# Twenty-two taps of a depthwise convolution moved from VectorE to GpSimd, beside a recurrence

## The chip, the cores and the metric

The kernel runs on one core of one Trainium2 chip. The metric is the device time of one execution in microseconds. Engine names are those of the profile: PE is TensorE, DVE is VectorE, ACT is ScalarE, POOL is GpSimd, SP is SyncE, which only issues transfers here.

## The reference

One inference layer for 512 prompt tokens and 8 sample tokens, width 1024. Cut to what matters here:

```python
z = x @ w_in
u = z_conv[..., :512] * sigmoid(z_conv[..., 512:])          # GLU, 512 channels
c = depthwise_causal_conv(u, conv_w, width 31) + conv_b     # the convolution of this case
c = silu(layer_norm(c))
...                                                         # r, k, v, decay, rate, gate from the other columns
S_t = S_{t-1} diag(w_t) + (S_{t-1} a_t) b_t^T + v_t k_t^T   # RWKV-7 recurrence, 8 heads of 64
y_t = S_t r_t
h = concat(c, groupnorm(y) and bonus, gated) @ w_out
x = layer_norm(ALPHA * x + h);  x = layer_norm(ALPHA * x + moe(x))   # 64 experts, top 8
```

## The kernel before

All data is float32. The kernel has two blocks of instructions per engine. In the first (`prepare`) the input projection, the GLU, the token shift and the keys are made, and a small triangular system is solved on DVE. In the second (`recur_and_mix`) the recurrence runs over 16 chunks of 32 tokens, then come the normalisations, the output projection, the routing and the 64 experts.

The convolution lies in four tiles of 128 channels (`m.conv[:, i]`), each with 31 taps over 512 positions. `Taps.take(count)` does the next `count` taps on DVE. Tap 0 of a tile is one `tensor_scalar` (times weight, plus bias, L174), each other tap one `scalar_tensor_tensor` that multiplies the shifted input by the weight and adds the sum so far (L176). Each waits for the one before it (`Chain.link`). Of the 124 taps, 74 are done in the first block, 19 at the start of the second (14, then `add_reads(0)`, then 5, then `add_reads(1)`), and these complete the third tile. The fourth tile's 31 taps are spread over the recurrence: three in each of steps 0 to 9, and the last one in step 10 (`TAPS_OVER`).

A step `n` of the recurrence on DVE is, in order: the old state times the chunk's decay (L2025), plus `moves` (L2027), then side work that the step's tables name (`add_reads` L1973, `centre` L1924 to L1926, `shift_late` L1965, the taps, parts of the sample's state L1983 to L1992, and so on), then the wait for PE's `step(n)` and the addition of its product (L2062), which raises `state_ready`. PE's `step(n)` (L1455) waits for the state before it. Behind it PE's queue holds, in an order written out by hand, two late projection columns (L1583, in steps 1 and 3), `push` (L1406), `solve` (L1415), `moves_of` (L1431 to L1443) and `outputs` (L1469 to L1478); ACT copies their results out of PSUM (L1704 to L1721) before DVE and PE can use them. In step 10 DVE also finishes the convolution of the 8 sample tokens, and in step 11 it folds the four tiles for the mean (L1930, L1931), for which PE waits in step 12.

POOL's queue in the second block begins with clearing the 42 semaphores of the first block; then it waits for the last `solve` (`w2_done`), makes two small masks (L1366 to L1371), and has nothing further to do before the mixing is over. SP's queue issues the load of `w_out` (L1284) after the last late column and the last `solve`.

`place(m, at, ...)` and `view(...)` name pieces of large SBUF areas; `m.AT_COL` is where the projection's four weight buffers lie, of which the late columns use the second and third, and `pushed` the first half of the fourth.

Of the kernel before, what the change touches and what calls it, by code (L numbers as in the profile page):

```python
# [19 lines left out]
ALU = mybir.AluOpType  # L20
# [3 lines left out]
P = 128  # L24
D = 1024
KD = D // P
T = 512
# [4 lines left out]
DC = 512  # L32
CT = DC // P
# [43 lines left out]
WB = 4  # L77
# [14 lines left out]
def par(name):  # L92
    return CW + PARAMS.index(name)
# [30 lines left out]
def place(m, at, *shape):  # L124

    size = 1
    for n in shape:
        size *= n
    assert at + size <= SLOTS * EXPERT_FLOATS
    names = "abcde"[:len(shape)]  # L130
    flat = m.w_exp[:, at:at + size]
    return flat.rearrange(f"p ({' '.join(names)}) -> p {' '.join(names)}", **dict(zip(names, shape)))


def view(t, at, *shape):

    size = 1
    for n in shape:
        size *= n
    names = "abcde"[:len(shape)]  # L140
    return t[:, at:at + size].rearrange(f"p ({' '.join(names)}) -> p {' '.join(names)}", **dict(zip(names, shape)))


def halves(ap):

    return ap.rearrange("p (b t) -> p b t", b=2)
# [858 lines left out]
def recur_and_mix(nc, m, ctx_out):  # L1005
# [12 lines left out]
    TURN = {14: 0}  # L1018
    SCALE = {9: 0, 13: 1, 15: 3}
    TAPS_OVER = 10  # L1020
    CONV = 11
    BIG = 1e30
    GONE = -3e38
    QD = D // 4
    with ExitStack() as ctx:
# [3 lines left out]
        def sem(name):  # L1029
            return ctx_out.enter_context(nc.semaphore(name))  # L1030
# [5 lines left out]
        st = place(m, m.UPPER, 32, N)  # L1036
        ln_scale = place(m, m.AT_LORA, TT)
        w1 = m.glu_sig[:, 0:DC]
        state = view(m.x_area, 0, RING, CT, N)
        pushed = place(m, m.AT_COL + (WB - 1) * KD * P, DC)  # L1040
        tail_rows = view(m.x_area, RING * CT * N + DC, 2, DC)[0:38]
# [79 lines left out]
        def early_sem(name):  # L1121
            m.spent_later.append(m.second_sems.enter_context(nc.semaphore(name)))
            return m.spent_later[-1]
# [30 lines left out]
        bonus_scaled = sem("bonus_scaled")  # L1154
        o_ready = sem("o_ready")
        final_stored = sem("final_stored")
        conv_folded = early_sem("conv_folded")
        mean_done = early_sem("mean_done")
        conv_centred = early_sem("conv_centred")
# [77 lines left out]
        def tail_width(t):  # L1237
            return sum(column(*SHIFTED[s])[1] for s in tail_columns(t))
# [11 lines left out]
        with nc.Block() as block:  # L1250
            @block.sync
            def _(sp):
# [15 lines left out]
                for t in range(5):  # L1268
# [4 lines left out]
                    else:  # L1273
                        c0, w = DC * (t - 1), tail_width(t)
# [5 lines left out]
                sp.dma_start(sample_y, m.scr_y).then_inc(sample_y_loaded, 16)  # L1280
                sp.wait_ge(row_taken, use["col", 2 * LATE - 1] + 1)
                sp.wait_ge(w2_done, TM)
                for c in range(2):
                    sp.dma_start(m.w_out_half[c][:], m.w_out[:, c * 512:(c + 1) * 512].rearrange("(k p) n -> p k n", p=P)).then_inc(m.w_out_loaded[c], 16)  # L1284
                sp.dma_start(router_w[:], m.router_w.rearrange("(k p) n -> p k n", p=P)).then_inc(loaded, 16)
# [73 lines left out]
            @block.gpsimd  # L1359
            def _(pool):  # L1360
                for spent in m.spent:
                    pool.sem_clear(spent)
                pool.sem_inc(spent_cleared)
                ch = Chain(pool, m.pool_step, m.pool_count)
                pool.wait_ge(w2_done, TM)
                nc.gpsimd.memset(before[:], 1.0)  # L1366
                ch.link(nc.gpsimd.memset(first[:], 1.0))

                nc.gpsimd.affine_select(out=before[:], in_=before[:], compare_op=ALU.is_gt, fill=0.0, base=0,
                                        pattern=[[1, P]], channel_multiplier=-1)  # L1370
                nc.gpsimd.affine_select(out=first[:], in_=first[:], compare_op=ALU.is_gt, fill=0.0, base=0,  # L1371
                                        pattern=[[1, G], [-1, G]], channel_multiplier=0).then_inc(routing_consts, 1)
                pool.wait_ge(mixed, NT)
                nc.gpsimd.memset(scores[:, TM, :], 0.0).then_inc(routing_consts, 1)  # L1374
                pool.wait_ge(sh_sig_ready, 1)
                ch.link(nc.gpsimd.tensor_tensor(sh_sig[:], sh_sig[:], sh_gate[:], ALU.mult))
                pool.wait_ge(sh_up_ready, 1)
                nc.gpsimd.tensor_tensor(sh_h[:, 0, :], sh_sig[:], sh_h[:, 0, :], ALU.mult).then_inc(sh_h_ready, 1)
                pool.wait_ge(sh_sig_ready, 2)
                ch.link(nc.gpsimd.tensor_tensor(sh_sig[:], sh_sig[:], sh_gate[:], ALU.mult))  # L1380
                for b in range(2):
                    pool.wait_ge(sh_up_ready, 2 + b)
                    half = slice(HALF * b, HALF * (b + 1))
                    nc.gpsimd.tensor_tensor(sh_h[:, 1, half], sh_sig[:, half], sh_h[:, 1, half], ALU.mult).then_inc(sh_h_ready, 1)
                pool.wait_ge(x1_stored, 16 * NT)
                pool.wait_ge(sh_done, 8)
                for q in range(NB):
                    gather(nc, m, pool, Job(q))
                work.gpsimd(pool)

            @block.tensor
            def _(pe):
# [200 lines left out]
                for n in range(NCH):  # L1593
                    j, c = n // CM, n % CM
                    step(n)
                    if n == CONV + 1:
                        pe.wait_ge(conv_folded, 1)
# [98 lines left out]
            def _(act):  # L1696
# [98 lines left out]
                for n in range(NCH):  # L1795
# [27 lines left out]
                    if n in SCALE:  # L1823
                        scale_bonus(SCALE[n])
                    if n == CONV + 3:
                        act.wait_ge(conv_centred, 1)
# [80 lines left out]
            def _(dve):  # L1907
                ch = Chain(dve, m.vector_step, m.vector_count)
# [60 lines left out]
                def add_reads(g):  # L1969

                    dve.wait_ge(move_taken, g + 1)
                    r = m.r_dec[:, :, N * g:N * (g + 1)].rearrange("p i (c t) -> p c i t", c=2)
                    tt(r, r, p_keep[:, :, :, N:], ALU.add).then_inc(read_taken, 1)  # L1973
# [45 lines left out]
                for n in range(NCH):  # L2019
                    j, c = n // CM, n % CM  # L2020
                    old, new = state[:, n % RING], state[:, (n + 1) % RING]
                    dve.wait_ge(state_ready, n + 1)
                    if n + 1 >= RING:
                        dve.wait_ge(y_done, (n + 1 - RING) // CM + 1)
                    ch.link(tt(new, old, m.chunk_decay[:, :, n:n + 1].broadcast_to([P, CT, N]), ALU.mult))  # L2025
                    dve.wait_ge(move_taken, n // 2 + 1)
                    ch.link(tt(new, new, moves[:, (n // 2) % SETS, n % 2, 1].rearrange("p (i n) -> p i n", i=CT), ALU.add))  # L2027
                    if c == 3 and j + 1 < TM:
                        add_reads(2 * j + 2)
                    if c == 0 and j >= 1:  # L2030
                        add_reads(2 * j + 1)
                    if n in INVERT:
                        invert(INVERT[n])
                    if n in FINISH:
                        finish_out(FINISH[n])
                    if n in CENTRE:
                        centre(CENTRE[n])
                    if n in SHIFT:
                        shift_late(SHIFT[n])
                    if n < TAPS_OVER:  # L2040
                        taps.take(min(3, CT * CW - m.taps_done))
                    if n < 2:
                        sample_reads(n)
                    elif n < 4:
                        sample_kept_part(n - 2)
                    elif n == 4:
                        sample_rows_out()
                    if n == TAPS_OVER:
                        taps.take(CT * CW - m.taps_done)
                        ch.link(tt(m.conv[:, :, T:TT], m.u_pad[:, :, CW - 1 + T:CW - 1 + TT], m.params[:, :, CW - 1:CW].broadcast_to([P, CT, B]), ALU.mult))  # L2050
                        ch.link(tt(m.conv[:, :, T:TT], m.conv[:, :, T:TT], m.conv_sum[:], ALU.add))
                    if n == CONV:
                        fold_chunks(m.conv)
                    if n == CONV + 2:
                        dve.wait_ge(mean_done, 1)
                        for i in range(CT):
                            last = tt(halves(m.conv[:, i, :]), halves(m.conv[:, i, :]), banks(p_sum), ALU.subtract)
                        last.then_inc(conv_centred, 1)
                    if n in SUM:
                        squares(SUM[n])  # L2060
                    dve.wait_ge(step_done, n + 1)
                    tt(new, new, pst[:], ALU.add).then_inc(state_ready, 1)  # L2062
# [75 lines left out]
                ch.link(nc.vector.tensor_tensor(sel_g, sel_g, keep_f, ALU.mult))  # L2138
                ch.link(nc.vector.tensor_scalar(grp[:], keep[:], 1.0, BIG, ALU.subtract, ALU.mult))
                ch.link(nc.vector.tensor_tensor(sel_g, sel_g, grp_f.unsqueeze(2).broadcast_to([P, NT * G, E // G]), ALU.add))  # L2140
# [838 lines left out]
```

## Time and profile before

| | us |
|---|---|
| median of 3 runs | 1148.97 |
| lowest and highest | 1143.69, 1150.23 |
| the profiled execution: its own time | 1149.05 |
| the profiled execution: its span | 1147.3 |
| start of the second block (PE's first instruction in it) | 221.5 |
| steps 0 to 7 of the recurrence on DVE | 240.48 to 287.14 |
| steps 8 to 15 on DVE | 287.14 to 328 |
| experts | 467 to 1111 |

The span is cut into stretches by time from its start. In a row of the timeline the first number is the start, the second the length of the instruction or of several alike in a row (x3), and the bracket behind it the time for which the engine had been idle before, and what ended it. On one engine the rows can overlap by some 0.08 us, since the end of an instruction overlaps the start of the next one.

### The profile page before, as it was taken

The numbers are of one execution on the slowest core, as the hardware profiler recorded it, in microseconds if no ns is written. First come the engines' busy times: TensorE is split into PE (matmuls) and PEld (weight loads), VectorE is DVE, ScalarE is ACT, GpSimd is POOL, SyncE is SP. The second block draws the span as 40 slices with busy tenths as digits, with TensorE's granted clock in tenths as the row PEclk, the third lists the DMA queues.
The fourth block names the chain that finished last, engine by engine and source line by source line (L and its number), as shares of the span: only waits on it lengthen the run. The fifth ranks groups of instructions, "written<-read, shape, count | busy, mean of one in ns | idle before, by whom it ended". The sixth has DMA issues, their size and how long they took to land.

```text
span 1147.3 us, 31310 instructions
## 1 busy us (share of the span) xinstructions
PE 1063.6 (93%) x13702; PEld 753.5 (66%) x13703; DVE 714.2 (62%) x1562; ACT 224.7 (20%) x472; POOL 320.9 (28%) x327
## 2 busy tenths in 40 slices
PE   7999998977889999999999999999999999999996
PEld 6877886755653577666666666666666666666662
DVE  0788869788674869755586455544454544555438
ACT  2146421222447121010011110011101011100113
POOL 2000010000000002454455444444444444444410
PEclk9998999979669999999999999999999999999998
DMA  7221131330435467699999999999999999999661
GB/s 214 74 56 38 54 93 42 75 120 5 161 101 199 148 233 297 240 363 367 359 366 367 380 360 356 377 350 359 370 360 357 361 361 356 365 372 350 184 180 76
DMA packets 91928, 282.44 MB, mean 246 GB/s; under 512 B 22494, under 2 KB 49631, under 8 KB 66949
## 3 DMA queue, kind: packets, MB, share of 16 engines
q1 hardware_dynamic: 74685, 243.55, 57.0%
q0 software_dynamic: 16160, 33.62, 11.9%
q10 hardware_dynamic: 944, 3.24, 0.8%
q8 instruction: 109, 1.79, 0.6%
q14 instruction: 30, 0.25, 0.1%
HBM read 260.93 MB, written 35.86 MB: 259 GB/s over the span
## 4 chain that ended last, share of the span: by engine, by line
PE 64%; DVE 9%; issue 4%; ACT 2%; DMA 1%; SPq 0%; DVEq 0%; POOLq 0%
PE ph L2364 32%; PE ph L2391 19%; PE ph L1542 2%; PE ph L1560 2%; PE pz_late L1583 1%; DVE w_exp L176 1%; PE ph L1683 1%; DMA w_exp<-scr_f 1%; DVE w_exp L2602 1%; PE pz_late L1500 1%; DVE w_exp L2594 1%; PE pz_late L1501 1%; DMA scr_f<-arena,row 1%; PE ph L1431 1%; PE pt L933 0%
## 5 line engine op out<-in xcount | busy, mean ns | idle before, releaser
L2364 PEld LDWEIGHTS ph<-arena,w_exp 128*64 128x64 f32 x8192 | 353.1, 138 | 103.2 <-issue 100.5
L2364 PE MATMUL ph<-arena,w_exp 128*64 128x96 f32 x8192 | 389.6, 248 | 30.6 <-issue 26.6
L2391 PE MATMUL ph<-w_exp,arena 128*96 128x512 f32 x512 | 234.6, 601 | 0.0
L977 POOL DMA_INDIRECT x_area<-scr_x,piece_row x192 | 203.4, 1060 | 82.8 <-issue 56.4
L2426 POOL DMA_INDIRECT scr_f<-arena,row x62 | 91.6, 1477 | 265.7 <-PE ph L2364 236.9
L523 PE MATMUL pz<-w_exp 128*128 128x260 f32 x672 | 159.0, 395 | 0.3 <-ACT w_exp L335 0.3
L2391 PEld LDWEIGHTS ph<-w_exp,arena 128*96 128x96 f32 x512 | 78.4, 162 | 109.9 <-issue 103.2
L523 PEld LDWEIGHTS pz<-w_exp 128*128 128x128 f32 x672 | 129.9, 196 | 23.7 <-issue 2.7
L2409 DVE TENSOR_SCALAR arena<-ph,row_weight 96x512 f32<-96x512 f32 x64 | 47.8, 747 | 130.8 <-PE ph L2391 130.8
L2379 DVE TENSOR_TENSOR arena<-arena,ph 128x192 f32<-128x192 f32 x64 | 22.5, 352 | 161.3 <-ACT arena L2372 161.3
L2372 ACT ACTIVATE arena<-ph 128x192 f32<-128x192 f32 x64 | 21.1, 330 | 479.9 <-PE ph L2364 464.8
L2349 DVE STREAM_TRANSPOSE arena<-x_area 128x768 f32<-128x768 f32 x64 | 102.5, 1601 | 3.2 <-DMA x_area<-scr_x,piece_row 2.0
L176 DVE SCALAR_TENSOR_TENSOR w_exp<-arena,w_exp 128x512 f32<-128x512 f32 x120 | 90.0, 750 | 3.6
L2401 ACT ACTIVATE arena<-ph,row_weight 96x512 f32<-96x512 f32 x64 | 43.6, 682 | 104.0 <-PE ph L2391 76.7
L1560 PE MATMUL ph<-w_exp 128*128 128x512 f32 x128 | 57.8, 604 | 0.0
L1560 PEld LDWEIGHTS ph<-w_exp 128*128 128x128 f32 x128 | 24.2, 194 | 29.5 <-issue 29.0
L955 DVE TENSOR_SCALAR piece_row<-found 32x3 uint32<-32x3 f32 x240 | 40.6, 169 | 4.4
L964 DVE COPY row_weight<-found 32x2 f32<-32x2 f32 x180 | 36.9, 205 | 3.1
L809 POOL COPY w_exp<-w_exp 128x8 f32<-128x8 f32 x4 | 2.6, 653 | 129.2 <-DVE w_exp L727 129.2
L922 DVE TENSOR_TENSOR arena<-slot_index,position 128x480 bf16<-128x480 f32 x60 | 38.4, 644 | 0.0
L1374 POOL MEMSET arena<- 128x64 f32 x1 | 0.2, 151 | 115.7 <-PE ph L1572 115.7
L1366 POOL MEMSET arena<- 128x128 f32 x1 | 0.2, 204 | 106.0 <-PE ph L1415 106.0
(384 smaller groups left out, 1016.7 us busy)
## 6 DMA issues: line engine op xcount, KB each, us to landing
w_exp<-in_exp_up_dram SPq DMA_DIRECT2D x64, 1024.0 KB
w_exp<-in_exp_down_dram SPq DMA_DIRECT2D x64, 1024.0 KB
w_exp<-in_exp_gate_dram SPq DMA_DIRECT2D x64, 1024.0 KB
w_exp<-in_w_in_dram SPq DMA_DIRECT2D x22, 512.0 KB, 3.9
w_exp<-in_x_prompt_dram SPq DMA_DIRECT2D x8, 512.0 KB, 5.4
w_exp<-in_w_out_dram SPq DMA_DIRECT2D x2, 2048.0 KB, 11.6
w_exp<-scr_f SPq DMA_DIRECT2D x8, 512.0 KB, 8.5
x_area<-scr_x,piece_row POOLq DMA_INDIRECT x192
```

Source lines behind the costliest of these rows:

```text
L176: self.ch.link(self.nc.vector.scalar_tensor_tensor(out, u, w, out, ALU.mult, ALU.add))
L523: last = nc.tensor.matmul(banks(pz[0:w, c % 2, :])[:, b, :], m.w_col[:, c % WB, k, 0:w], halves(m.x_t[:, k, :])[:, b, :], start=(k == 0), ...
L922: nc.vector.tensor_tensor(m.members[:, e], m.slot_index[:].unsqueeze(1).broadcast_to([P, NT, CAP]), src.unsqueeze(2).broadcast_to([P, NT, ...
L955: last = nc.vector.tensor_scalar(m.piece_row[32 * quad:32 * (quad + 1), s, :], m.found[rows, :, 0], float(QUADS), float(QUADS * TT + quad) ...
L977: nc.gpsimd.indirect_dma_start(m.x_pieces[:, s, r, :], None, m.scr_x1.rearrange("t (q c) -> (t q) c", q=QUADS), bass.IndirectOffsetOnAxis( ...
L1560: last = nc.tensor.matmul(ph[0:n, i % 2, c * 512:(c + 1) * 512], lhs, w_out[c][:, kw, :], start=(part == 0 and k == 0), stop=(part == 1 an ...
L2349: nc.vector.transpose(x_list_t[:, s % 2].rearrange("p k (r t) -> p r k t", r=RUNS), m.x_pieces[:, s].rearrange("p r (c k) -> p r k c", k=K ...
L2364: last = nc.tensor.matmul(pgu[64 * half:64 * half + 64, s % 2, (2 * part + j) * CAP:(2 * part + j + 1) * CAP], w[job.slot][:, k, f0:P * ha ...
L2391: last = nc.tensor.matmul(pyl[0:CAP, c, :], hid[:, s % 2, j, :], m.expert_down[job.slot][:, j, c * 512:(c + 1) * 512], start=(j == 0), sto ...
L2401: nc.scalar.activation(y_list[:, s % 2, 0:512], pyl[0:CAP, 0, :], ACT.Copy, scale=row_weight[0:CAP, job.l, 1:2]).then_inc(y_act, 1)
L2409: nc.vector.tensor_scalar(y_list[:, s % 2, 512:1024], pyl[0:CAP, 1, :], row_weight[0:CAP, job.l, 1:2], None, ALU.mult).then_inc(y_dve, 1)
L2426: nc.gpsimd.indirect_dma_start(m.scr_f[copy_of(q)], bass.IndirectOffsetOnAxis(ap=row[:, job.l:job.l + 1], axis=0), y_list[:, s % 2, :], No ...
```

## The change

POOL does the first 22 taps of the fourth tile, in the second block, before its wait for `w2_done`. A tap is two instructions there: a `tensor_scalar` into one of two buffers (`tap_product`, in the first weight buffer, which is free by then), and a `tensor_tensor` that adds this to the sum. Tap 0 is one `tensor_scalar`. DVE takes no taps in steps 0 to 7; in steps 8, 9 and 10 it takes three each, after a wait in step 8 for all 22. SP's load of `w_out` waits for them too, since it overwrites the buffers.

```diff
@@ recur_and_mix
     TAPS_OVER = 10
+    POOL_OVER = (8, 9)
     CONV = 11
+    LAST_TILE = CT - 1
+    POOL_TAPS = 22
+    PRODUCTS = 2
...
+        tap_product = [place(m, m.AT_COL + at, T) for at in (0, T, (WB - 1) * KD * P + DC)][0:PRODUCTS]
...
+        taps_added = sem("taps_added")
... SP's queue
                 sp.wait_ge(w2_done, TM)
+                sp.wait_ge(taps_added, POOL_TAPS)
                 for c in range(2):
                     sp.dma_start(m.w_out_half[c][:], ...)
... POOL's queue
                 pool.sem_inc(spent_cleared)
                 ch = Chain(pool, m.pool_step, m.pool_count)
+                sums = m.conv[:, LAST_TILE, 0:T]
+                for k in range(POOL_TAPS):
+                    u, w = m.u_pad[:, LAST_TILE, k:k + T], m.params[:, LAST_TILE, k:k + 1]
+                    if k == 0:
+                        bias = m.params[:, LAST_TILE, par("conv_b"):par("conv_b") + 1]
+                        nc.gpsimd.tensor_scalar(sums, u, w, bias, ALU.mult, ALU.add).then_inc(taps_added, 1)
+                    else:
+                        product = tap_product[k % PRODUCTS]
+                        ch.link(nc.gpsimd.tensor_scalar(product, u, w, None, ALU.mult))
+                        pool.wait_ge(taps_added, k)
+                        nc.gpsimd.tensor_tensor(sums, sums, product, ALU.add).then_inc(taps_added, 1)
                 pool.wait_ge(w2_done, TM)
... DVE's queue, step n
-                    if n < TAPS_OVER:
+                    if n in POOL_OVER:
+                        if n == POOL_OVER[0]:
+                            dve.wait_ge(taps_added, POOL_TAPS)
+                            m.taps_done += POOL_TAPS
                         taps.take(min(3, CT * CW - m.taps_done))
```

## Rows read from the trace of the kernel before

**Rows 1.** Windows: busy us and instructions of each engine, PE's clock, DMA share.

```profile
core 0: us, PE busy (x) PEld busy (x) DVE busy (x) ACT busy (x) POOL busy (x), PEclk, DMA share, GB/s
221.50:240.40 18.90, 16.25 (x388) 13.99 (x392) 15.10 (x23) 5.38 (x12) 0.00 (x0) 0.92 0.70 227
240.40:287.10 46.70, 36.35 (x984) 26.04 (x974) 42.98 (x72) 11.84 (x24) 0.00 (x0) 0.83 0.03 6
...
467.00:1100.00 633.00, 602.39 (x8742) 422.06 (x8735) 336.24 (x890) 64.08 (x128) 286.65 (x248) 1.00 0.97 346
```

**Rows 2.** Timeline of DVE, from the second block's start to step 0.

```profile
221.99 10.89 DVE L176 SCALAR_TENSOR_TENSOR w_exp<-arena,w_exp 128x512 f32<-128x512 f32 x14
234.87 0.42 DVE L1973 TENSOR_TENSOR w_exp<-w_exp,ph 128x256 f32<-128x256 f32 x1 [1.99 <-ACT w_exp L1721]
235.21 3.90 DVE L176 SCALAR_TENSOR_TENSOR w_exp<-arena,w_exp 128x512 f32<-128x512 f32 x5
240.14 0.42 DVE L1973 TENSOR_TENSOR w_exp<-w_exp,ph 128x256 f32<-128x256 f32 x1 [1.04 <-ACT w_exp L1721]
```

**Rows 3.** Timeline of DVE, steps 1, 4, 8 and 11.

```profile
247.43 2.33 DVE L176 SCALAR_TENSOR_TENSOR w_exp<-arena,w_exp 128x512 f32<-128x512 f32 x3
...
251.06 1.22 DVE L1984 TENSOR_REDUCE arena<-arena 128x16 f32<-128x1024 f32 x1
...
269.11 0.42 DVE L1973 TENSOR_TENSOR w_exp<-w_exp,ph 128x256 f32<-128x256 f32 x1 [1.64 <-ACT w_exp L1721]
...
288.41 0.42 DVE L1973 TENSOR_TENSOR w_exp<-w_exp,ph 128x256 f32<-128x256 f32 x1 [0.39 <-ACT w_exp L1721]
...
305.98 0.42 DVE L2062 TENSOR_TENSOR x_area<-x_area,pst 128x256 f32<-128x256 f32 x1 [1.96 <-PE pst L1455]
```

**Rows 4.** Timeline of PE: the late column of step 3, and step 11.

```profile
260.73 5.38 PE L1583 MATMUL pz_late<-w_exp 128*32 128x260 f32 x16
...
304.83 1.12 PE L1455 MATMUL pst<-x_area,w_exp 64*64 64x64 f32 x16 [4.35 <-issue]
```

**Rows 5.** Groups of POOL's instructions by shape: busy us, mean ns, idle before.

```profile
L2780 POOL TENSOR_SCALAR_AFFINE_SELECT w_exp<-w_exp 128x128 f32<-128x128 f32 x3 | 0.9, 311 | 0.2
...
L2767 POOL MEMSET arena<- 128x512 f32 x1 | 0.5, 517 | 0.0
...
L2786 POOL TENSOR_SCALAR_AFFINE_SELECT is_token<-is_token 128x1 f32<-128x1 f32 x1 | 0.2, 186 | 0.0
```

**Rows 6.** Timeline of POOL: shared expert, beside DVE's work.

```profile
433.28 1.28 POOL L1376 TENSOR_TENSOR arena<-arena 128x520 f32<-128x520 f32 x1 [19.03 <-ACT arena L1883]
...
448.21 1.16 POOL L1384 TENSOR_TENSOR arena<-arena 128x260 f32<-128x260 f32 x1 [2.24 <-ACT arena L1890]
451.65 0.73 POOL L1384 TENSOR_TENSOR arena<-arena 128x260 f32<-128x260 f32 x1 [2.28 <-ACT arena L1890]
```

**Rows 7.** Timeline of DVE: two collisions, and a small TENSOR_TENSOR in step 2.

```profile
256.78 0.23 DVE L1990 TENSOR_TENSOR arena<-arena 128x64 f32<-128x64 f32 x1
...
433.57 1.08 DVE L2127 TENSOR_TENSOR arena<-arena 128x40 f32<-128x40 f32 x1
...
448.06 0.71 DVE L2165 TENSOR_TENSOR arena<-arena,table 128x320 f32<-128x320 f32 x1
```

**Rows 8.** Timeline of POOL: small copies of the first block, then its first mask.

```profile
79.75 0.65 POOL L809 COPY w_exp<-w_exp 128x8 f32<-128x8 f32 x1 [70.14 <-DVE w_exp L727]
80.35 0.66 POOL L810 COPY w_exp<-w_exp 128x8 f32<-128x8 f32 x1
...
81.54 0.18 POOL L813 COPY w_exp<-w_exp 128x8 f32<-128x8 f32 x1
...
297.51 0.20 POOL L1366 MEMSET arena<- 128x128 f32 x1 [105.97 <-PE ph L1415]
```

**Rows 9.** Timeline of DVE beside those copies.

```profile
79.68 0.67 DVE L732 TENSOR_TENSOR w_exp<-w_exp,arena 128x496 f32<-128x496 f32 x1
80.27 0.69 DVE L734 TENSOR_TENSOR x_area<-w_exp 128x512 f32<-128x512 f32 x1
```

## The prediction

> **What bounds the kernel now.** I read the windows first. From 467 us on PE is busy for 602 of 633 us at full granted clock [rows 1], and that stretch starts when everything before it is done, so a time gained or lost earlier is gained or lost at the end, one for one. The change lies in two windows. From 221.5 to 240.4 us DVE is busy for 15.1 of 18.9 us, and from 240.4 to 287.1, steps 0 to 7, for 42.98 of 46.7; PE has 36.35 there, at a mean clock of 0.83, and POOL has nothing [rows 1]. So DVE is what limits steps 0 to 7, and POOL is free.
>
> The timeline of DVE shows where that time goes. Ahead of step 0 stand 14 and 5 taps with two waits for ACT behind them, 1.99 and 1.04 us [rows 2]. In a step the three taps are 2.33 us of some 6 [rows 3]. DVE's waits inside the stretch are few: 1.64 us in step 4, behind the late column of step 3 on PE [rows 3, 4], and 0.39 at the start of step 8 [rows 3]. In step 11 DVE waits 1.96 us for PE, which itself had stood idle for 4.35 us for no cause that the profile names ("issue") [rows 3, 4].
>
> **What is removed.** Steps 0 to 7 held 24 taps; step 10 goes from one to three. A tap costs its start-to-start distance, 10.89/14 = 0.78 us [rows 2]. So 24 x 0.78, less 0.2 for the shorter first one, is 18.5 us off DVE in steps 0 to 7, and 2 x 0.78 = 1.6 us on in step 10, at most. If nothing else happened, the gain could not be 18.5: PE's 36.35 us of work in that window leave 10.3 of the 46.7 [rows 1], and the taps now cover PE and ACT's work in steps 3 and 7, whose waits would grow.
>
> **What is added on POOL.** 22 one-input multiplications and 21 additions with two inputs, of 128x512. An addition of 128x520 alone took 1.28 us, one of 128x260 0.73 [rows 6], so 2.1 ns per element and 0.18 fixed: 1.26 us for 512. For the multiplication there is no row. Below it lies the memset of 512, 0.52 us; above it the two-input addition, 1.26. Nearest is the affine select, one input and one output as well: 0.31 us for 128 elements against 0.19 for one, 0.98 ns per element, so 0.19 + 512 x 0.98 = 0.69 [rows 5]. I take 0.65 to 0.7, and keep both ends. Alone the chain is 22 x 0.68 + 21 x 1.26 + 43 x 0.06 for the links = 44 us. POOL starts behind 42 semaphore clears, for which no row has a price: nothing, or at most 42 x 0.19 (the smallest instruction in [rows 5]), 8 us. I take 1.5, so a start at 223, and an end at 267 if it met no one. DVE reaches step 8 at 287, so its wait there is 20 us away, and SP's wait for the taps stays hidden too: the last `solve`, for which it waits anyway, ends at 297.5 [rows 8].
>
> **What the two engines do to each other.** This is the part that decides. In the shared expert POOL's addition ran from 433.28 to 434.56 [rows 6]. DVE's TENSOR_TENSOR of only 40 elements, started at 433.57, took 1.08 us and ended at 434.65 [rows 7]; one of 64 elements takes 0.23 [rows 7]. It stood until POOL was done. The other way round, DVE had a TENSOR_TENSOR from 448.06 to 448.77 [rows 7] and POOL's addition of 260 elements, started at 448.21, took 1.16 us instead of 0.73 [rows 6]. So the two exclude each other for nearly the whole of an instruction. Who wins in a row of DVE instructions is in the first block: copies of 8 elements on POOL take 0.18 us alone and 0.65 and 0.66 beside DVE, each ending as one DVE instruction ends [rows 8, 9]. They take turns; neither starves. After a turn some 0.15 us of the waiting instruction's fixed part is already over, as the 1.08 us above shows (0.09 left after POOL's end, against 0.23).
>
> A tap on DVE is a SCALAR_TENSOR_TENSOR with two inputs in SBUF; no row shows that form beside POOL. By the nearest rows it is blocked as TENSOR_TENSOR is; the bound below is that it is not blocked at all. The Trainium skill says more than these rows (SBUF — State Buffer, Who interferes with whom): any VectorE instruction with two SBUF inputs contends with a GpSimd instruction that reads SBUF, whichever starts first keeps the port for its whole length, and a reduce does not contend. By that rule taps would be blocked and the sum below would stand; were only TENSOR_TENSOR blocked, the first term of it would be gone. On the multiplication's price the skill (GPSIMD Engine Reference, Engine selection) calls one-input work roughly line rate, with which the row of the affine select agrees.
>
> **The sum.** When each met instruction takes turns, POOL's hold the way for their length less some 0.15 us: 0.5 for a multiplication, 1.1 for an addition, 0.8 on average; DVE gets back 0.15 of it. So a DVE instruction with two SBUF inputs is 0.65 us later for each POOL instruction it meets.
> - Up to step 0: 18 of the 19 taps meet one, 18 x 0.65 = 11.7 us, less the 3.03 us that DVE waited for ACT anyway: step 0 starts 8.7 us later, with about 20 of POOL's 43 done.
> - Steps 0 to 7: 18.5 us of taps gone. The other 23 POOL instructions meet some 28 two-input instructions of DVE, but where DVE reduces one input (1.22 us, once in each of steps 0 to 3 [rows 3]), reads PSUM or waits, they cost nothing; I take two in three as met, 15 x 0.65 = 10 us. The waits behind the late columns in steps 3 and 4, formerly covered by taps, come to some 3 us. Net -5.5.
> - Start of step 8: PE's and ACT's moves, which step 7's taps had covered, now show; the 0.39 us wait becomes about 2, +1.5.
> - Step 10: 1.6 us, which PE's 4.35 us pause in step 11 should hide, since DVE waits 1.96 us for it [rows 3, 4]. 0, or 1.6 if the pause moves.
> - PE, waiting longer before step 0, starts from the lower of its two clocks more often; it was at a mean of 0.83 already [rows 1]. +1, from nothing to 3.
>
> 8.7 - 5.5 + 1.5 + 0 + 1 = +5.7, say +6. The profiled execution took 1149.05 us, by 1.75 more than its span and within 0.1 of the median. So 1155.
>
> **The rivals.**
> - *Less met, or a cheap multiplication* (0.52 us, the memset's row, or a later start of POOL): the multiplications hold 0.15 less, 22 x 2/3 x 0.15 = 2.2 us, a start 4 us later leaves some 5 collisions fewer ahead of step 0, 3 us. Together +1: 1150. It shows as step 0 at 245 or earlier.
> - *A dear multiplication*, as long as an addition, 1.26: 0.55 more in each, 22 x 0.55 = 12 us on POOL, of which some two thirds are met: +8. The chain is then 56 us alone and, with some 15 us of waiting for DVE, ends at 294, so that DVE also stands at step 8. +14: 1163. Against it: the affine select.
> - *No collision with taps* (other side). If SCALAR_TENSOR_TENSOR leaves POOL its way, the 8.7 us ahead of step 0 don't arise, POOL is half through by step 0, and steps 0 to 7 give what PE leaves, 10.3 at most, less 1.5 at step 8 and what the steps' own TENSOR_TENSORs lose. -8 at best, -6 likely: 1142. It decides from this: a loss ahead of step 0 under 3 us, which is the slack there. Against it: both collisions in the trace.
>
> **Chances.** About 0.5% or 5.7 us is what a measurement of this kernel can tell from no change. Forecast (+3 to +9): 0.50, about half of it beyond the bound. Less met (-3 to +3): 0.16. Dear multiplication (+9 to +16): 0.22. No collision with taps (-10 to -3): 0.12. So faster 0.10, same 0.41, slower 0.49. The likeliest case's own range is 1152 to 1158; the range that holds eight in ten runs from 1145 to 1163.
>
> **What would show it.** Right: DVE's 14 taps from 222 us stretch from 10.9 to about 20 us, their mean near 1.4; step 0 starts near 249; a POOL addition in there takes 1.5 to 1.9 us, start to end; POOL is done near 280, without DVE waiting for it at step 8; step 8 starts 3 us later than before, the experts 5 to 6 later. Wrong: taps at 0.75 us beside POOL, or POOL's multiplications over 1 us where DVE is idle, or step 8 starting before 285. If the loss is there ahead of step 0 but the experts start no later, then the steps had more to give than I allowed.

## The result, and the profile after

| | median us (executions) | against the kernel before, same chip |
|---|---|---|
| before | 1148.69 (20), from 1143.69 to 1152.32 | |
| changed | 1153.12 (20), from 1148.65 to 1156.61 | 1.0042 [1.0029, 1.0055] |

The change makes the kernel slower by 0.42%, 4.8 us at 1148.69 (the two medians themselves are 4.4 us apart); forecast were 1155 us and +6. The size was right. The sum behind it was not: its first term was four to five times too large, and a wait of 6 us that it denied made up for that. That the two nearly cancel is in good part luck.

The profiled execution took 1155.57 us, its span 1153.6. The windows of the changed kernel: the stretch ahead of step 0, steps 0 to 7, and the experts (columns as in [rows 1]).

```profile
221.12:242.30 21.18, 18.84 (x435) 15.76 (x436) 20.34 (x23) 5.70 (x13) 17.35 (x11) 0.85 0.62 203
242.30:282.20 39.90, 31.32 (x839) 22.25 (x841) 31.48 (x49) 10.88 (x23) 38.90 (x26) 0.88 0.03 6
467.30:1117.80 650.50, 613.75 (x8989) 432.81 (x8988) 337.64 (x892) 64.44 (x129) 289.05 (x249) 1.00 0.96 341
```

The block starts at 221.12, so step 0 is 21.2 us behind it, where it was 19.0 [rows 1]. POOL began only 11 instructions in that time. Steps 0 to 7 take 39.9 us instead of 46.7; POOL is busy for all of it and DVE no longer is: 31.48 us against 42.98. The timeline of DVE, ahead of step 0 and in step 8:

```profile
221.61 14.89 DVE L176 SCALAR_TENSOR_TENSOR w_exp<-arena,w_exp 128x512 f32<-128x512 f32 x14
236.54 0.42 DVE L1991 TENSOR_TENSOR w_exp<-w_exp,ph 128x256 f32<-128x256 f32 x1
236.88 5.09 DVE L176 SCALAR_TENSOR_TENSOR w_exp<-arena,w_exp 128x512 f32<-128x512 f32 x5
242.00 0.42 DVE L1991 TENSOR_TENSOR w_exp<-w_exp,ph 128x256 f32<-128x256 f32 x1
242.34 1.03 DVE L2043 TENSOR_TENSOR x_area<-x_area 128x256 f32<-128x256 f32 x1
...
282.18 0.42 DVE L2043 TENSOR_TENSOR x_area<-x_area 128x256 f32<-128x256 f32 x1
282.64 0.42 DVE L2045 TENSOR_TENSOR x_area<-x_area,w_exp 128x256 f32<-128x256 f32 x1
286.46 0.42 DVE L1991 TENSOR_TENSOR w_exp<-w_exp,ph 128x256 f32<-128x256 f32 x1 [3.40 <-ACT w_exp L1739]
292.90 2.33 DVE L176 SCALAR_TENSOR_TENSOR w_exp<-arena,w_exp 128x512 f32<-128x512 f32 x3 [6.02 <-POOL w_exp L1382]
...
296.32 0.43 DVE L2043 TENSOR_TENSOR x_area<-x_area 128x256 f32<-128x256 f32 x1
```

L2043 is the first instruction of a step (L2025 before). The 14 and 5 taps grew from 10.89 and 3.90 us [rows 2] to 14.89 and 5.09, and both waits for ACT between them are gone. Step 8 lasts 14.1 us (5.0 before): DVE waits 3.40 us for ACT (0.39 in [rows 3]), then 6.02 us for POOL's last addition. The timeline of POOL, at its start and at its end:

```profile
224.53 0.76 POOL L1377 TENSOR_SCALAR w_exp<-arena 128x512 f32<-128x512 f32 x1 [35.21 <-issue]
225.28 2.00 POOL L1380 TENSOR_SCALAR w_exp<-arena 128x512 f32<-128x512 f32 x1
227.36 1.48 POOL L1382 TENSOR_TENSOR w_exp<-w_exp 128x512 f32<-128x512 f32 x1
228.83 1.99 POOL L1380 TENSOR_SCALAR w_exp<-arena 128x512 f32<-128x512 f32 x1
230.90 1.50 POOL L1382 TENSOR_TENSOR w_exp<-w_exp 128x512 f32<-128x512 f32 x1
...
289.96 1.56 POOL L1380 TENSOR_SCALAR w_exp<-arena 128x512 f32<-128x512 f32 x1
291.60 1.27 POOL L1382 TENSOR_TENSOR w_exp<-w_exp 128x512 f32<-128x512 f32 x1
```

The last rows fall in DVE's wait, so they are the prices without company: 1.27 us for the addition, as forecast, and 1.56 for the multiplication, where I had 0.65 to 0.7. Beside taps it is 2.00. Tap 0 multiplies and adds in one instruction and takes 0.76. Single taps on DVE, and pairs of them (x2), where the second row of a pair starts with the second tap:

```profile
222.30 0.75 DVE L176 SCALAR_TENSOR_TENSOR w_exp<-arena,w_exp 128x512 f32<-128x512 f32 x1
...
229.43 1.06 DVE L176 SCALAR_TENSOR_TENSOR w_exp<-arena,w_exp 128x512 f32<-128x512 f32 x1
...
230.52 2.43 DVE L176 SCALAR_TENSOR_TENSOR w_exp<-arena,w_exp 128x512 f32<-128x512 f32 x2
...
231.31 2.74 DVE L176 SCALAR_TENSOR_TENSOR w_exp<-arena,w_exp 128x512 f32<-128x512 f32 x2
```

The one at 222.30 met nothing. The one at 229.43 began and ended inside POOL's multiplication from 228.83 to 230.82 and was held for 0.31 us. The next began at 230.52, and the one after it, which the last row names, at 231.31, inside the addition from 230.90 to 232.40. That one ended at 230.52 + 2.43 = 232.95, 1.64 us after its start: held for 0.89. By the Trainium skill (SBUF — State Buffer, Who interferes with whom) whichever of two such instructions starts first keeps the port for its whole length. The addition agrees, with one tap read. The multiplication does not: by the rule the tap at 229.43 would have ended after 230.82, and it ended at 230.49.

### The profile page after: what moved, and what is told of

Same layout as the page of the kernel before. It is cut to its first block, busy times and chain, and to the rows that moved or that the text cites. A ratio compares the mean times of both kernels' runs of the same rounds, so it can differ in the third digit from the quotient of the medians.

```text
span 1153.6 us, 31349 instructions
## 1 busy us (share of the span) xinstructions
PE 1063.3 (92%) x13702; PEld 754.2 (65%) x13703; DVE 709.0 (61%) x1540; ACT 224.7 (19%) x472; POOL 387.8 (34%) x370
## 4 chain that ended last, share of the span: by engine, by line
PE 60%; DVE 7%; POOL 6%; issue 4%; ACT 1%; DMA 1%; POOLq 0%; SPq 0%; DVEq 0%
PE ph L2385 32%; PE ph L2412 19%; POOL w_exp L1380 3%; POOL w_exp L1382 3%; PE ph L1560 2%; PE ph L1578 2%; PE ph L1701 1%; DMA w_exp<-scr_f 1%; DVE w_exp L176 1%; DVE w_exp L2623 1%; PE pz_late L1518 1%; DMA scr_f<-arena,row 1%; DVE w_exp L2615 1%; PE pz_late L1519 1%; PE pt L933 0%
## 5 line engine op out<-in xcount | busy, mean ns | idle before, releaser
L176 DVE SCALAR_TENSOR_TENSOR w_exp<-arena,w_exp 128x512 f32<-128x512 f32 x99 | 79.4, 802 | 9.1 <-POOL w_exp L1382 6.0
L1380 POOL TENSOR_SCALAR w_exp<-arena 128x512 f32<-128x512 f32 x21 | 35.3, 1683 | 0.0
```

The costliest lines, as they stand in the source:

```text
L176: self.ch.link(self.nc.vector.scalar_tensor_tensor(out, u, w, out, ALU.mult, ALU.add))
L1380: ch.link(nc.gpsimd.tensor_scalar(product, u, w, None, ALU.mult))
```

## The experiments

Ratios are to the kernel before on the same chip, with 95% intervals. They are not the quotients of the two medians, from which they differ by up to 0.0015. The first four ran in one set (before: 1140.88 us, 29 executions), the next four in a second (1081.74, 35), the last two in a third (1147.78, 23). "From the block's start" counts from PE's first instruction of the second block.

**Both kernels again.** No edit. The two recorded traces can't be the whole story: the experts start at 467.5 in one and at 467.3 in the other.

> The kernel before, unchanged, as a control of what two equal kernels show, and a second profile of it. The recorded traces of before and after stand 0.25 us apart at the start of the experts (467.6 and 467.4 us), and 6.3 us apart at the end. Theory A (the loss is made in the recurrence and handed on) has no place for that, unless one of the two traces is an odd one. Theory C (the experts' stretch differs by some us between executions of one kernel, so that the two traces fell apart by chance there) expects the stretch from the first to the last gate-up multiplication of the experts, 644.0 us in the trace of before, to come out elsewhere here, by 2 us or more, with the start of the experts again within 0.5 us of 467.6. Theory B (the changed program makes the experts slower) expects 644 again, within 1 us. All expect a ratio of 1.000, within 0.2%.

> The changed kernel, unchanged, for a second trace. Ratio 1.003 to 1.0055 again. The start of the experts: theory A expects 3 to 6 us later than before in this trace; B and C expect within 1 us of 467.4. The experts' stretch, 650.4 us in the first trace: B expects 649 to 651 again, C anything from 643 to 651.

before_again: 1139.38 us, 0.9993 [0.9971, 1.0015]. after_again: 1147.37, 1.0050 [1.0032, 1.0067]. The groups of the experts' matmul, with the times from its first to its last, in before, before_again, after and after_again, in this order:

```profile
L2364 PE MATMUL ph<-arena,w_exp x8192: 242/246/302, 467.5 to 1111.5; 128*64 128x96 f32 x200
```
```profile
L2364 PE MATMUL ph<-arena,w_exp x8192: 242/246/302, 458.5 to 1102.5; 128*64 128x96 f32 x200
```
```profile
L2385 PE MATMUL ph<-arena,w_exp x8192: 242/246/302, 467.3 to 1117.8; 128*64 128x96 f32 x200
```
```profile
L2385 PE MATMUL ph<-arena,w_exp x8192: 242/246/301, 466.5 to 1110.4; 128*64 128x96 f32 x200
```

The experts took 644.0, 644.0, 650.5 and 643.9 us. So the recorded pair puts the whole loss into the experts, which the change doesn't touch; it is a difference between executions, since after_again doesn't have it, and two later kernels do (650.6, 650.3). From the block's start to the experts the four took 246.0, 240.1, 246.2 and 246.2. The first is the odd one: from the start of step 11 to that of step 13 it needed 15.5 us, before_again 9.6. PE's pause of 4.35 us [rows 4] lies there, but before_again has one of 3.32 us too, a step later, so most of this difference has no cause that I can name. None of the three theories had the experts of one kernel start 6 us apart in two traces. The second pair is the one to read, since its ends agree with the ratios:

| from the block's start, us | step 0 | step 8 | step 9 | step 11 | experts |
|---|---|---|---|---|---|
| before_again | 19.6 | 64.7 | 70.3 | 79.4 | 240.1 |
| after_again | 21.2 | 61.1 | 75.3 | 84.8 | 246.2 |
| difference | +1.6 | -3.6 | +5.0 | +5.4 | +6.1 |

The 6.1 us stand beside 0.0050 x 1140.88 = 5.7 from all executions.

**The 22 taps left out.** Nobody computes them; DVE's sum of the fourth tile starts with tap 22.

```diff
-            if j == 0:
+            if j == 0 or (i, j) == (CT - 1, 22):
...
-                 for k in range(POOL_TAPS): ...      # and both waits for taps_added
```

> The 22 taps are not computed at all, neither on POOL nor on DVE; DVE starts the fourth tile's sum with tap 22. All else is as in the changed kernel, without the waits for POOL. This is the most that freeing DVE can bring. Theory A, with PE's work as the floor of steps 0 to 7: step 8 starts 9 to 10 us earlier than before, and the end 7 to 9 us earlier (ratio 0.992 to 0.994). Rival, from the changed kernel's trace, in which step 8 begins 5 us early and yet PE's pause in step 11 and the copies of ACT behind it have taken up all but 1.1 us of a 4 us delay by step 15: part of an advance is lost in the same places, and the end comes 3 to 6 us earlier (0.995 to 0.9975).

1135.19 us, 0.9938 [0.9916, 0.9959]. The windows of before_again in steps 0 to 7, and then of this kernel ahead of step 0 and in steps 0 to 7:

```profile
238.00:283.10 45.10, 34.35 (x929) 24.75 (x924) 42.95 (x73) 11.86 (x24) 0.00 (x0) 0.84 0.03 6
```
```profile
219.94:239.60 19.66, 17.27 (x431) 14.55 (x432) 15.18 (x23) 5.39 (x12) 0.00 (x0) 0.91 0.64 219
239.60:277.00 37.40, 30.55 (x842) 21.93 (x845) 25.17 (x48) 11.13 (x23) 0.00 (x0) 0.91 0.03 7
```

This is the most that this distribution of the taps can gain: 7.1 us (0.62% of 1140.88, from 4.7 to 9.6 by the interval; the medians are 5.7 apart). Taking 17.8 us of work off DVE (42.95 to 25.17) shortens steps 0 to 7 by 7.7; DVE's idle time there grows from 2.1 to 12.2 us. It waits for PE and ACT. Step 8 starts 7.6 us earlier than in before_again (57.1 from the block's start), which is less than the 9 to 10 of the theory with PE's work as the floor, although the end came where that theory had it; the interval reaches into the rival's range.

**The 22 taps done twice.** POOL does its taps into a scratch buffer that nobody reads; DVE does all 31 in their old steps, and waits for POOL in step 11 only.

```diff
-                sums = m.conv[:, LAST_TILE, 0:T]
+                sums = place(m, m.AT_COL + (WB - 1) * KD * P + DC, T)
...
-                    if n in POOL_OVER: ...
+                    if n < TAPS_OVER:
```

> POOL does the same 22 taps into a scratch buffer, and DVE does all 31 of its own as in the kernel before: collisions without the relief. DVE waits for POOL only in step 11. From the changed kernel's trace a tap that meets POOL's addition takes 1.65 us and one that meets its multiplication 1.06, against 0.75, while POOL's multiplication takes 1.56 us even alone. Theory A (collisions cost as predicted, 0.65 us for each instruction of POOL): 43 x 0.65 = 28 us less what is hidden, step 8 15 to 25 us later, end 15 to 25 us later (1.013 to 1.022). Theory from the trace (0.9 for an addition, 0.3 for a multiplication, but only some two in three met): 21 x 0.9 + 22 x 0.3 = 25 x 2/3 = 17 us less 3 of slack ahead of step 0: step 8 some 12 to 14 us later, end 9 to 14 us later (1.008 to 1.012).

1156.88 us, 1.0143 [1.0112, 1.0174]: 16.3 us. Step 0 is 21.2 us from the block's start and step 8 81.9, against 19.6 and 64.7 in before_again. Nobody waits for POOL before step 11, so the 17.2 us are the delay that POOL's instructions bring to a DVE that is hardly ever idle. DVE's busy time up to step 8 grew by 20.8 us (58.09 to 78.89), and 3.6 of that fell into its waits. POOL is done at 295.1, ahead of step 8 at 300.2. The 22 taps cost DVE itself 22 x 0.78 = 17.2. The expectation worked out from the trace (12 to 14 us at step 8) was too low: it took two in three instructions as met, and 20.8 us over 43 instructions is 0.48 for every one of them. The prediction's price of 0.65 with its range of 15 to 25 us held.

**The multiplication with a second operation.** Times weight, plus 0.0; the same values.

```diff
-                        ch.link(nc.gpsimd.tensor_scalar(product, u, w, None, ALU.mult))
+                        ch.link(nc.gpsimd.tensor_scalar(product, u, w, 0.0, ALU.mult, ALU.add))
```

> The changed kernel, with POOL's multiplications written as the first one is, multiply and then add (here add 0.0), instead of multiply alone. In the changed kernel the first, of the two-step form, took 0.76 us and the 21 others 1.56 us even where DVE was idle. If the form is what makes them long (theory L), they take 0.7 to 0.8 us alone, POOL's chain ends 15 us earlier, near 60 us after the block's start instead of 72, DVE does not wait for POOL in step 8, and the 6.0 us of that wait go: ratio to the kernel before 0.998 to 1.001. Rival: the length is that of any one-input tensor_scalar of this size, and the first was short for another reason; then 1.5 us again, the wait of 6 us stays, ratio 1.005.

1084.00 us, 1.0006 [0.9981, 1.0031]. The groups of POOL's instructions, of the changed kernel and then of this one:

```profile
L1380 POOL TENSOR_SCALAR w_exp<-arena 128x512 f32<-128x512 f32 x21 | 35.3, 1683 | 0.0
L1382 POOL TENSOR_TENSOR w_exp<-w_exp 128x512 f32<-128x512 f32 x21 | 30.9, 1471 | 1.8
```
```profile
L1382 POOL TENSOR_TENSOR w_exp<-w_exp 128x512 f32<-128x512 f32 x21 | 33.1, 1578 | 1.7
L1380 POOL TENSOR_SCALAR w_exp<-arena 128x512 f32<-128x512 f32 x21 | 19.1, 909 | 0.0
```

One more operation makes it shorter by 0.77 us. POOL is done before step 8, and the wait of 6 us is gone. Ahead of step 0, however, POOL now gets through more of its list: step 0 is 24.5 us from the block's start, 3.3 later than in the changed kernel, and step 8 66.5, 5.4 later. In this trace most of the wait is paid there instead: step 9 comes only 1.7 us earlier (73.6 against 75.3). The ratios, 1.0006 against 1.0042 and 1.0050, put the gain at some 4 to 5 us; this profiled execution took 1089.32 us, 5.3 above the median, so how much of the wait is paid back stays open.

**18 taps on POOL.** DVE takes four, four and five in steps 8 to 10.

```diff
-    POOL_TAPS = 22
+    POOL_TAPS = 18
-                        taps.take(min(3, CT * CW - m.taps_done))
+                        taps.take(min(4, CT * CW - m.taps_done))
```

> The changed kernel, but POOL does 18 taps and DVE 13, four each in steps 8 and 9 and five in step 10, with the wait for POOL in step 8 as it was. If the wait at step 8 is what costs (POOL needs 2.9 us for each tap, more than DVE's 0.78), POOL is done 11 us earlier, the wait of 6.0 us is gone, DVE has 4 x 0.78 = 3.1 us more: end 2 to 3.5 us earlier than the changed kernel, ratio to before 1.002 to 1.003. If the collisions were the cost (the prediction's theory), four taps less for POOL save 8 instructions x 0.65 = 5 us of collisions, and 3.1 us come back on DVE: 1.003 too; the two differ in where the time goes, the wait in step 8 or the starts of steps 0 to 8.

1083.41 us, 1.0022 [0.9997, 1.0048]. The timeline of DVE in step 8 shows the wait for ACT alone:

```profile
283.15 0.42 DVE L1991 TENSOR_TENSOR w_exp<-w_exp,ph 128x256 f32<-128x256 f32 x1 [1.95 <-ACT w_exp L1739]
283.49 3.11 DVE L176 SCALAR_TENSOR_TENSOR w_exp<-arena,w_exp 128x512 f32<-128x512 f32 x4
```

The interval doesn't tell this kernel from before, and hardly from the changed one.

**The products alone.** POOL makes 22 products that nobody reads; DVE does all 31 taps.

```diff
+                    nc.gpsimd.tensor_scalar(tap_product[k % PRODUCTS], u, w, None, ALU.mult).then_inc(taps_added, 1)
-                        nc.gpsimd.tensor_tensor(sums, sums, product, ALU.add).then_inc(taps_added, 1)
```

> POOL does only the 22 multiplications, into the two buffers, and no additions; DVE does all 31 taps of its own as before. It prices what one-input work on POOL takes from DVE. If a POOL instruction holds DVE's two-input work for its whole length (1.56 us each), DVE is late by up to 22 x 1.4 = 30 us, step 8 by 20 or more, ratio 1.015 to 1.025. If it holds it only while it reads, as the taps of 1.06 us in the changed kernel's trace suggest (0.3 us over 0.75), 22 x 0.3 = 6.6 us, less 3 us of slack ahead of step 0: step 8 some 3 to 4 us later, ratio 1.002 to 1.004, and no tap over 1.1 us.

DVE waits for POOL in step 11 only. 1085.58 us, 1.0033 [1.0008, 1.0058]. The group of the multiplication, and the timeline of DVE ahead of step 0:

```profile
L1375 POOL TENSOR_SCALAR w_exp<-arena 128x512 f32<-128x512 f32 x22 | 38.7, 1759 | 35.1 <-issue 33.2
```
```profile
217.91 12.46 DVE L176 SCALAR_TENSOR_TENSOR w_exp<-arena,w_exp 128x512 f32<-128x512 f32 x14
232.81 4.64 DVE L176 SCALAR_TENSOR_TENSOR w_exp<-arena,w_exp 128x512 f32<-128x512 f32 x5
```

38.7 us of multiplications cost the kernel 3.6, with step 8 at 69.6 from the block's start (64.7 in before_again). The 14 and 5 taps grow by 1.6 and 0.7 us, against 4.0 and 1.2 with the additions. So the additions do most of the harm (16.3 us for both kinds, 3.6 for this one).

**Own sums.** POOL takes taps 9 to 30 into a buffer of its own, DVE taps 0 to 8, spread over the steps in which it had stood idle (one in step 3, two each in 5, 7, 8 and 9), and adds the two sums in step 10. So nobody waits for POOL before step 10.

```diff
-    POOL_OVER = (8, 9)
+    SPREAD = {3: 1, 5: 2, 7: 2, 8: 2, 9: 2}
...
+                    taps.take(SPREAD.get(n, 0))
... step 10
+                        dve.wait_ge(taps_added, POOL_TAPS)
+                        tt(m.conv[:, LAST_TILE, 0:T], m.conv[:, LAST_TILE, 0:T], pool_sum, ALU.add).then_inc(taps_joined, 1)
```

> Each engine sums its own taps: POOL taps 9 to 30 into a buffer of its own, DVE taps 0 to 8 in steps where it waited for ACT or PE (1 in step 3, 2 each in steps 5, 7, 8 and 9), and one addition joins the two in step 10. The same work for POOL as in the changed kernel, and nine taps for DVE, but no wait before step 10 and no taps bunched behind it. If the changed kernel's loss is the wait in step 8 and what stands behind it, it should come out ahead of the kernel before by a part of what leaving the taps out gave (0.9938): POOL done at 72 us after the block's start, step 10 not before 76, so no wait. I expect 0.996 to 0.999. If collisions are the loss, they are all still there, and it is 1.002 or more.

> The kernel of own_sums once more, beside the next one. It had a ratio of 0.9965 to the kernel before; if that is the kernel's and not that chip's, the ratio is 0.994 to 0.999 here too.

1078.17 us, 0.9965 [0.9946, 0.9984], and in the third set 1144.69, 0.9975 [0.9951, 1.0000]. It is the only one with all taps that comes out faster than before, by 0.25 to 0.35%, about 3 to 4 us; the second interval reaches no change. Its timeline of DVE in steps 7 and 8 (third set):

```profile
280.48 0.42 DVE L1993 TENSOR_TENSOR w_exp<-w_exp,ph 128x256 f32<-128x256 f32 x1 [1.54 <-ACT w_exp L1741]
280.81 1.53 DVE L176 SCALAR_TENSOR_TENSOR w_exp<-arena,w_exp 128x512 f32<-128x512 f32 x2
...
285.54 0.42 DVE L1993 TENSOR_TENSOR w_exp<-w_exp,ph 128x256 f32<-128x256 f32 x1 [0.94 <-ACT w_exp L1741]
285.88 2.31 DVE L176 SCALAR_TENSOR_TENSOR w_exp<-arena,w_exp 128x512 f32<-128x512 f32 x2
```

The wait for ACT of 3.40 us is down to 0.94, and no wait for POOL follows. Step 9 is 70.5 us from the block's start, where after_again has 75.3 and before_again 70.3. So the traces show the gain over the changed kernel, and not the one over the kernel before: in the two traces of own sums step 11 is at 79.6 and 79.8 (79.4 in before_again), and the experts at 242.7 and 238.0 (246.0 and 240.1 in the two of before). That gain rests on the medians and ratios alone.

**Own sums with the short multiplication.** Both edits together.

> own_sums with POOL's multiplication in its form with two operations (times weight, plus 0.0), which took 0.91 us where the form with one took 1.68. Theory one, what a POOL instruction costs DVE is not its length but a fixed hold, about 0.3 us for a multiplication and 0.9 for an addition: since nobody waits for POOL in own_sums, a shorter chain brings nothing, and because POOL then issues more of its instructions ahead of step 0, step 0 starts 1 to 3 us later and the ratio to the kernel before is 0.995 to 1.001, no better than own_sums. Theory two, POOL's length is what costs: 21 x 0.7 us = 15 us less of POOL's work, half of it beside DVE, would make it 3 to 7 us faster than own_sums, a ratio of 0.990 to 0.994.

1149.37 us, 1.0017 [0.9999, 1.0036], beside 0.9975 [0.9951, 1.0000] for own sums alone. The timelines of DVE ahead of step 0, of own sums and then of this kernel:

```profile
219.27 14.81 DVE L176 SCALAR_TENSOR_TENSOR w_exp<-arena,w_exp 128x512 f32<-128x512 f32 x14
...
234.45 5.09 DVE L176 SCALAR_TENSOR_TENSOR w_exp<-arena,w_exp 128x512 f32<-128x512 f32 x5
```
```profile
218.31 16.32 DVE L176 SCALAR_TENSOR_TENSOR w_exp<-arena,w_exp 128x512 f32<-128x512 f32 x14
...
235.01 6.83 DVE L176 SCALAR_TENSOR_TENSOR w_exp<-arena,w_exp 128x512 f32<-128x512 f32 x5
```

POOL's multiplications fell from 37.7 to 20.0 us in all, and the kernel became slower than own sums by 0.0042 x 1147.78 = 4.8 us: the profiled executions' spans differ by 4.8 too (1143.2, 1148.0), their experts by 0.3 only. Of this the recurrence shows 3.0 at step 11 (82.8 from the block's start against 79.8, and 79.6 in the other trace of own sums); the rest lies where the two traces of own sums differ by 4.7 themselves. The theory by which POOL's length is what costs had this kernel 3 to 7 us faster, and falls. Up to step 10 DVE is busy for 70.44 us here and for 67.70 in own sums, although POOL is busy for 53 us and not 69. What POOL costs DVE goes with the number of pairs that are met, not with POOL's busy time. POOL issues a pair every 3.55 us with the long form (225.28 to 228.83 in its timeline of the changed kernel) and every 2.77 with the short one, by its timeline in this kernel:

```profile
221.89 1.12 POOL L1382 TENSOR_SCALAR w_exp<-arena 128x512 f32<-128x512 f32 x1
223.09 1.58 POOL L1384 TENSOR_TENSOR w_exp<-w_exp 128x512 f32<-128x512 f32 x1
224.66 1.12 POOL L1382 TENSOR_SCALAR w_exp<-arena 128x512 f32<-128x512 f32 x1
```

In the changed kernel, from POOL's start at 224.53 to step 0, the 19 taps meet (242.0 - 224.5)/3.55 = 4.9 pairs and lose 5.2 us, 1.06 a pair; here, from POOL's start at 221.22, (241.9 - 221.2)/2.77 = 7.5 pairs and 8.4 us, 1.12 a pair.

## Why the prediction came out

- **Ahead of step 0, +8.7: wrong, measured +1.6 (second pair) to +2.2 (recorded pair).** This is the term that failed, by its count. The price held: 5.2 us over some 10 instructions met is 0.53 each, where I had 0.65. The count did not: 10 and not 18, since the multiplication took 2.00 us beside taps and POOL started at 224.53 and not 223. The slack of 3.03 us went as forecast. By kind the price was 0.35 for a multiplication and 0.95 for an addition (0.5 and 1.1, less the 0.15 that DVE gets back); measured are 0.31 and 0.89. For the multiplication that is luck: the price was to follow its length, I had the length at less than half of what it is, and by the same rule one of 2.00 us would have cost 1.7.
- **The price of the multiplication, 0.65 to 0.7 us: wrong, 1.56 alone.** The affine select [rows 5] was the nearest row and misled; it has the length of the form with two operations (0.76 for tap 0), not of the bare product. The Trainium skill (GPSIMD Engine Reference, Engine selection) calls one-input work roughly line rate. Beside DVE's own one-input tap 0 of 0.55 us that is near for the form with two operations (0.70 alone), and not for the bare product, which takes 2.8 times as long. The upper end that I kept, 1.26, was still below it.
- **Steps 0 to 7, -5.5: right in sum, wrong in both parts.** Between the second pair it is -5.2. The collisions, put at 10, cost 2.5 (39.9 us against 37.4 with the taps left out), since part of POOL's hold fell into time in which DVE would have waited anyway (its busy time grew by 6.3, from 25.17 to 31.48). The waits that the taps had covered, put at 3, cost some 10 (DVE's idle time of 2.1 grew to 12.2 with the taps left out). I had both numbers in hand: PE's work left 10.3 us, and 18.5 us of taps can't give more than about that.
- **Start of step 8, +1.5 and no wait for POOL: wrong, +8.6.** The wait for ACT grew by 3.0, more than I allowed, and then came 6.02 for POOL. This was the rival of the dear multiplication, with its end of POOL at 294 (measured: 292.87); its price of +14 came with collisions that weren't there. With the taps left out, step 8 takes 6.4 us and not 14.1.
- **Step 10, 0: about right.** From step 9 to step 11 +0.4 us (70.3 to 79.4, 75.3 to 84.8); in the recorded pair it is +1.4, near its other bound. But the pause that was to hide it belonged to the one execution that was recorded; in before_again it comes a step later.
- **PE's clock, +1: not seen.** Its mean is 0.85 ahead of step 0 and 0.88 in steps 0 to 7 of the changed kernel, 0.92 and 0.83 in [rows 1], 0.87 and 0.84 in before_again. Its +1 stands beside 1.1 us behind step 9 that I can't assign.
- **No collision with taps: fell.** Its own bound was a loss ahead of step 0 below 3 us, and the loss of 1.6 to 2.2 meets it; but the taps did grow by 5.2 us, and the rest of that filled the slack. The bound was badly chosen: it should have been the taps' own length.
- **The rivals were kept apart, and two of them came together.** Step 0 at 242.3 is the sign of the rival with less met, and POOL's end at 292.87 that of the dear multiplication. No case of the prediction had both.

The measured terms, 1.6 - 5.2 + 8.6 + 1.1 for all that follows, give 6.1 in this pair; forecast were 8.7 - 5.5 + 1.5 + 1. The first was forecast 7 too high and the third 7 too low, in part for one reason: a slower POOL collides less ahead of step 0 and ends later. The kernel with the second operation shows how large that part is. Its multiplication has the forecast length, and step 0 is 4.9 us later than in before_again (24.5 against 19.6): 3.3 of the 7 come from the slow multiplication, the rest I put to POOL's late start, a price somewhat below 0.65 and a slack of 3.63 us instead of 3.03.

What stays open: why the bare product takes twice as long as product and sum, how much of own sums' gain over the changed kernel comes from the missing wait and how much from where DVE's taps lie, and why the experts take 644 us in some executions and 650.5 in others.

## What to carry to other kernels

Moving work to POOL beside a DVE that is full of two-input instructions gained nothing in this kernel: 22 taps on POOL delayed DVE by as much (17.2 us) as doing them there would (17.2). It paid only as far as POOL's instructions fell into DVE's waits, so bound the gain first by the kernel without the work (7.1 us faster here), keep the meeting place late, in a sum of its own, and count the instructions that are met rather than POOL's busy time. And take a second trace of the same kernel before one stretch is blamed: two executions of one kernel differed by 6 us in the recurrence, and two of another by 6.5 us in the experts.

## What the runs showed of the hardware

- POOL's `tensor_scalar` of 128x512 takes 1.56 us alone with a multiplication only, and about 0.7 with a multiplication and an addition; in the trace of the kernel with the second operation, with DVE waiting or reading PSUM:

```profile
272.45 0.70 POOL L1380 TENSOR_SCALAR w_exp<-arena 128x512 f32<-128x512 f32 x1
```

- A tap on DVE ran inside POOL's multiplication and was 0.31 us longer; behind an addition it stood until that was over (0.89 us). Over all 43 instructions the loss was 0.48 us each (taps done twice).
- POOL's first instruction came 3.4 us after the block's start (221.12 to 224.53). The 42 semaphore clears stand ahead of it in its queue; that they are what took this time is not shown, since no run leaves them out.
- The second set of runs had the whole kernel at 1081.74 us, where the others had 1140.88 and 1147.78. The group of the experts' matmul, in the kernel with the second operation, shows where:

```profile
L2385 PE MATMUL ph<-arena,w_exp x8192: 246/246/302, 468.5 to 1048.4; 128*64 128x96 f32 x200
```

The experts took 579.9 us instead of 644; the recurrence ahead of them was no faster. The kernel of own sums needed 578.6 us for them in the second set and 650.6 in the third, both on a chip with the number 7, so it is not a matter of the kernel. Its cause is open.
